# The last expert pass of a two-layer backbone step: written out, its block kept on chip and summed through fp32 weight matrices

## The reference

```python
logits = h @ router_w + router_b
top_val, top_idx = lax.top_k(logits, 2)
top_w = softmax(top_val)
for e in range(8):
    out = out + combine[..., e:e+1] * swiglu(h, w_gu[e], w_down[e])
x = layer_norm(alpha * x + gate * out, g, b)
```

## Time and profile before

| | us |
|---|---|
| median of 3 runs (1509.24 to 1511.29) | 1509.93 |
| the profiled execution | 1505.81 |
| its span, first to last instruction | 1504.2 |
| pass 7, last matmul ends | 1453.6 |
| VectorE's last instruction ends | 1497.0 |

### The profile page before, as it was taken

The page is one execution under the profiler, slowest core; times in us unless marked ns, Lnnn a source line. Parts: engine busy times, 40 slices in busy tenths (PEclk is TensorE's granted clock), DMA queues, the critical chain, the costliest instruction groups (busy, mean ns, idle before and its releaser), DMA issues.

```text
span 1504.2 us, 20810 instructions
## 1 busy us (share of the span) xinstructions
PE 1377.2 (92%) x6907; PEld 1138.0 (76%) x6907; DVE 912.4 (61%) x1197; ACT 731.1 (49%) x1125; POOL 196.9 (13%) x264
## 2 busy tenths in 40 slices
PE   6899888999999989998889999999999999999960
PEld 2766467999999879986557788888888878877850
DVE  1325557633333386225875797555557999999967
ACT  1323545233333343323444684445446888888851
POOL 1000002500000032004320725000000000000013
PEclk9899989999999999999999899999999999999985
DMA  9885553884444415446655799766667999999922
GB/s 337 264 273 199 195 185 106 298 267 125 127 126 127 131 51 143 111 165 225 240 168 169 252 387 334 244 191 228 187 190 242 374 382 379 378 381 374 378 77 90
DMA packets 255249, 342.21 MB, mean 228 GB/s; under 512 B 16927, under 2 KB 210749, under 8 KB 255053
## 3 DMA queue, kind: packets, MB, share of 16 engines
q1 hardware_dynamic: 241210, 299.55, 60.4%
q0 software_dynamic: 12688, 41.72, 7.4%
q10 hardware_dynamic: 1282, 0.04, 0.0%
HBM read 318.65 MB, written 21.55 MB: 226 GB/s over the span
## 4 chain that ended last, share of the span: by engine, by line
PE 79%; DVE 11%; ACT 4%; issue 3%; DMA 3%; SPq 1%; POOL 0%; DVEq 0%; ACTq 0%; POOLq 0%
PE PS L2061 25%; PE PS L478 15%; PE PS L2068 12%; PE PS L467 6%; PE PS L468 6%; PE PS L469 6%; DVE wlo L453 2%; PE PS L597 2%; PE PS L2036 1%; DMA raw<-in_ada_w 1%; ACT BIG L1493 1%; DVE X L772 1%; DVE BIG L767 1%; DVE stats L774 1%; PE PS L622 1%
## 5 line engine op out<-in xcount | busy, mean ns | idle before, releaser
L453 DVE TENSOR_TENSOR wlo<-raw,whi 128x1024 fp32r<-128x1024 f32 x130 | 172.2, 1351 | 230.4 <-ACT whi L450 230.0
L1926 DVE TENSOR_TENSOR wlo<-BIG,whi 128x1024 fp32r<-128x1024 f32 x192 | 239.2, 1260 | 70.7 <-ACT whi L1922 69.2
L1922 ACT ACTIVATE whi<-BIG 128x1024 fp32r<-128x1024 f32 x192 | 202.7, 1060 | 68.3 <-PE PS L2061 42.0
L2061 PE MATMUL PS<-whi,Hh 128*128 128x512 f32 x560 | 224.0, 400 | 2.3 <-DVE Hl L1983 2.2
L2061 PE MATMUL PS<-whi,Hl 128*128 128x512 f32 x560 | 219.6, 392 | 0.0
L2061 PE MATMUL PS<-wlo,Hh 128*128 128x512 f32 x560 | 219.6, 392 | 0.0
L467 PE MATMUL PS<-Hh,whi 128*128 128x384 f32 x608 | 206.8, 340 | 10.1 <-DVE Hl L757 6.5
L1926 DVE TENSOR_TENSOR wlo<-raw,whi 128x1024 fp32r<-128x1024 f32 x150 | 184.2, 1239 | 48.6 <-ACT whi L1922 47.0
L468 PE MATMUL PS<-Hl,whi 128*128 128x384 f32 x608 | 205.3, 338 | 0.0
L469 PE MATMUL PS<-Hh,wlo 128*128 128x384 f32 x608 | 205.1, 337 | 0.0
L1922 ACT ACTIVATE whi<-raw 128x1024 fp32r<-128x1024 f32 x150 | 158.5, 1059 | 58.7 <-PE PS L2068 32.3
(11 more groups left out here) (354 smaller groups left out, 1949.0 us busy)
## 6 DMA issues: line engine op xcount, KB each, us to landing
raw<-in_moe_w_gu SPq DMA_DIRECT2D x224, 256.0 KB, 5.9
BIG<-in_moe_w_gu SPq DMA_DIRECT2D x224, 256.0 KB, 6.0
raw<-in_ada_w SPq DMA_DIRECT2D x96, 512.0 KB, 4.5
BIG<-in_moe_w_down SPq DMA_DIRECT2D x80, 512.0 KB, 7.3
raw<-in_ffn_w_gu SPq DMA_DIRECT2D x44, 512.0 KB, 3.9
raw<-in_w_in_c SPq DMA_DIRECT2D x32, 512.0 KB, 3.9
raw<-in_moe_w_down SPq DMA_DIRECT2D x32, 512.0 KB, 7.2
scr_tok<-BIG POOLq DMA_DIRECT2D x29, 512.0 KB, 9.3
```

Of the source, the lines that this page charges most:

```text
L453: self.eng.tensor_tensor(wlo[:, s, :], raw[:, s, :], whi[:, s, :].bitcast(f32), ALU.subtract).then_inc(lo_made, 1)
L1922: act.activation(whi[:, slot(v), :], moe_raw(v), ACT.Copy).then_inc(hi_made, 1)
L1926: dve.tensor_tensor(wlo[:, slot(v), :], moe_raw(v), whi[:, slot(v), :].bitcast(f32), ALU.subtract).then_inc(lo_made, 1)
L2061: last = pe.matmul(PS[:, 6 * b + c % 2, :], lhs, wt[:, s, 512 * k:512 * k + 512], start=(q == 0 and k == 0 and lhs is h and wt is whi), st ...
```

## The change

The last single pass (n) leaves the loop and is written out for every engine, and its 128 results never go to DRAM. What it computes is the same.

- `pool_table` also computes for each token copy its place relative to the last block (`slf`): at least `FAR` if it lies in that block, less if not. Five more GpSimd instructions, ahead of those that make `ctl`.
- `pool_pick`, on GpSimd ahead of the loop of single passes: `e2` is the weight of each copy that lies in another block, and zero otherwise; `pick_n` is per tile a 128x128 matrix of weights from the token to its row of the last block. In the last pass TensorE transposes the three matrices (unit 20) and ScalarE copies them to `pick` (unit 22).
- In the last pass nothing is fetched, no tokens are transposed or split, and the last six splits are left out.
- Once the block of pass n-1 is stored, GpSimd gathers five of the six tiles of rows, during the last pass; the sixth when its buffer (a ring buffer) has been read. Rows that lie in the last block are multiplied by the zero in `e2`.
- ScalarE weights tile 0, 1, 2 at units 33, 36, 38 (`act_weight`). VectorE does `mix_step` (weighted add, gate, ALPHA-add into X) one or two at a time at units 36 to 41, behind the other work of the unit, and the last two steps after the pass.
- The last block's result is read from PSUM twice: by ScalarE as it is (`yb[0]`, for the context tile) and by VectorE times the latent gate (`yg`). Six fp32 matmuls of 512 columns bring it to the tokens (`pick` x `yb` or `yg`), and `last_sum` adds it to X from PSUM. The sum of the other rows is in X already.
- `last_norm`: the whole normalisation on VectorE, as two scalar-tensor-tensor instructions per tile (tile 2 in two halves, each stored by itself). GpSimd has no part in the end.

```diff
@@ buffers
-        Yg = area([128, TT, 2, D], 3072)
+        pick_n = area([128, TT, 128], 1536)
+        pick = area([128, TT, 128], 16088)
+        pick_tmp = area([128, 128])
+        Yg = [[hsn[0], hsn[1]], [yb[1], gate_bc[:, 0, 0, :]], [gate_bc[:, 0, 1, :], xraw[0]]]
+        yg = xraw[2]
@@ pool_table
+            ch.step(pool.tensor_scalar(over, cd, 256.0, -FAR, ALU.mult, ALU.add))
+            ch.step(pool.tensor_scalar(over2, cs, 128.0, None, ALU.mult))
+            ch.step(pool.tensor_tensor(over, over, over2, ALU.add))
+            for kk in range(2):
+                last = pool.tensor_tensor(slf[:, :, kk:kk + 1], wk[:, kk, :, 0:1],
+                                          over[:, 7:8].unsqueeze(1).to_broadcast([128, TT, 1]), ALU.subtract)
+            ch.step(last)
@@ new
+        def pool_pick(pool, ch):
+            ch.step(pool.tensor_scalar(e2, slf, FAR, None, ALU.is_lt))
+            ch.step(pool.tensor_tensor(e2, e2, wts[:, :, :], ALU.mult))
+            for t in range(TT):
+                for kk, dst in ((0, pick_n[:, t, :]), (1, pick_tmp)):
+                    last = pool.tensor_scalar(dst, C("iota_far"), slf[:, t, kk:kk + 1], wts[:, t, kk:kk + 1],
+                                              ALU.is_equal, ALU.mult)
+                ch.step(last)
+                ch.step(pool.tensor_tensor(pick_n[:, t, :], pick_n[:, t, :], pick_tmp, ALU.add))
+            pool.sem_inc(route_step, 1)
@@ act_pass
-                act_unit_hi(act, w + RING, p)
+                if not last or w + RING < UB:
+                    act_unit_hi(act, w + RING, p)
+                if last and w == 22:
+                    act.wait_ge(route_step, 7)
+                    act.activation(pick.rearrange("p t n -> p (t n)"), PS[:, 4, 0:TT * 128], ACT.Copy
+                                   ).then_inc(route_step, 1)
+                if last and w in (33, 36, 38):
+                    act_weight(act, (33, 36, 38).index(w))
...
+            if last:
+                act.wait_ge(yb_free[0], p + 1)
+                act.activation(yb[0][:, 0:512], PS[:, 2, :], ACT.Copy).then_inc(last_raw, 1)
+                act.wait_ge(last_gated, 1)
+                act.activation(yb[0][:, 512:D], PS[:, 3, :], ACT.Copy).then_inc(last_raw, 1)
+                return
@@ dve_pass
-                dve_unit_lo(dve, w + RING, p)
+                if not last or w + RING < UB:
+                    dve_unit_lo(dve, w + RING, p)
+                if last and w >= UB - RING:
+                    for i in LAST_MIX[w - UB + RING]:
+                        mix_step(dve, ch, i // 3, i % 3)
...
+            if last:
+                dve.wait_ge(unit_used, p * UB + (U_MOE + UB))
+                dve.tensor_tensor(yg[:, 512:D], PS[:, 3, :], gate_bc[:, 1, 0, 512:D], ALU.mult).then_inc(last_gated, 1)
+                dve.wait_ge(last_raw, 1)
+                dve.tensor_tensor(yg[:, 0:512], PS[:, 2, :], gate_bc[:, 1, 0, 0:512], ALU.mult).then_inc(last_gated, 1)
+
+        LAST_MIX = ((0,), (1,), (2, 3), (4,), (5,), (6,))
+
+        def mix_step(dve, ch, t, i):
+            y = Yg[t][0]
+            if i == 0:
+                dve.wait_ge(y_mixed, t + 1)
+                ch.step(dve.scalar_tensor_tensor(y, Yg[t][1], e2[:, t, 1:2], y, ALU.mult, ALU.add))
+            elif i == 1:
+                ch.step(dve.tensor_tensor(y, y, gate_bc[:, 1, 1 if t == 0 else 0, :], ALU.mult))
+            else:
+                dve.wait_ge(x_done, 2 * TT + t + 1)
+                ch.step(dve.scalar_tensor_tensor(X[:, t, :], X[:, t, :], ALPHA, y, ALU.mult, ALU.add))
+
+        def last_sum(dve, ch, t):
+            dve.wait_ge(y_summed, t + 1)
+            src = PS[:, (4, 6, 0)[t]:(4, 6, 0)[t] + 2, :].rearrange("p a n -> p (a n)")
+            if t == 0:
+                ch.step(dve.tensor_tensor(Yg[0][0], src, gate_bc[:, 1, 1, :], ALU.mult))
+                src = Yg[0][0]
+            ch.step(dve.tensor_tensor(X[:, t, :], X[:, t, :], src, ALU.add))
+            for half in range(2):
+                last = dve.bn_stats(stats[:, t, half, :], X[:, t, 512 * half:512 * half + 512])
+            ch.step(last)
+            dve.bn_aggr(mv[:, t, :], stats[:, t, :, :].rearrange("p a b -> p (a b)")).then_inc(var_made, 1)
+
+        def last_norm(dve, ch, t, cols):
+            dve.wait_ge(rstd_made, TT * 3 + t + 1)
+            for lo, hi in cols:
+                x = X[:, t, lo:hi]
+                ch.step(dve.scalar_tensor_tensor(x, x, mv[:, t, 0:1], lng[:, lo:hi], ALU.subtract, ALU.mult))
+                dve.scalar_tensor_tensor(x, x, rstd[:, t:t + 1], lnb[:, lo:hi], ALU.mult, ALU.add).then_inc(x_done, 1)
@@ pe_pass and pe_experts
+                if final and w == 20:
+                    pe.wait_ge(route_step, 6)
+                    for t in range(TT):
+                        last = pe.transpose(PS[:, 4, 128 * t:128 * t + 128], pick_n[:, t, :], C("ident"))
+                    last.then_inc(route_step, 1)
...
-            with pe.Fori(n2 + 1, n + 1) as p:
+            with pe.Fori(n2 + 1, n) as p:
                 pe_pass(pe, p, False, (0,), n2)
+            pe_pass(pe, n, False, (), n2, final=True)
+            pe.wait_ge(route_step, 8)
+            for t, bank, y in ((0, 4, yb[0]), (1, 6, yg), (2, 0, yg)):
+                for half in ((0, 1) if t == 0 else (1, 0)):
+                    if t == 0:
+                        pe.wait_ge(last_raw, half + 1)
+                    elif t == 1:
+                        pe.wait_ge(last_gated, 2 - half)
+                    last = pe.matmul(PS[:, bank + half, :], pick[:, t, :], y[:, 512 * half:512 * half + 512],
+                                     start=True, stop=True)
+                last.then_inc(y_summed, 1)
@@ pool_experts
+            pool_pick(pool, ch)
-            with pool.Fori(n2 + 1, n + 1) as p:
+            with pool.Fori(n2 + 1, n) as p:
...
+            for t in range(TT - 1):
+                for kk in range(2):
+                    gather(t, kk)
+            gather(TT - 1, 0)
+            pool.wait_ge(lo_made, n * UB + (S_MOE + UB - MRING + RING + 1))
+            pool.sem_inc(pool_pass, 1)
+            gather(TT - 1, 1)
@@ tail_dve
-            dve_norm_sum(dve, ch, 3, 0, mixed(dve, ch, 0))
-            dve_norm_sum(dve, ch, 3, 1, mixed(dve, ch, 1))
-            dve_norm_scale(dve, 3, 0)
-            dve_norm_sum(dve, ch, 3, 2, mixed(dve, ch, 2))
-            dve_norm_scale(dve, 3, 1)
-            dve_norm_scale(dve, 3, 2)
...
+            mix_step(dve, ch, 2, 1)
+            mix_step(dve, ch, 2, 2)
             dve.wait_ge(ln_in, 32 * 4)
+            last_sum(dve, ch, 0)
+            last_sum(dve, ch, 1)
+            last_norm(dve, ch, 0, OUT_COLS[0])
+            last_sum(dve, ch, 2)
+            last_norm(dve, ch, 1, OUT_COLS[1])
+            last_norm(dve, ch, 2, OUT_COLS[2])
@@ tail_pool
-            pool_norm(pool, ch, 3)
```

More of the change, by code:

```diff
@@ L1689, in backbone_step @@
         y_mixed = sem("y_mixed")
-        x_last = sem("x_last")
+        last_raw = sem("last_raw")
+        last_gated = sem("last_gated")
+        y_summed = sem("y_summed")
         pool_pass = sem("pool_pass")
@@ L1902, in sp_experts @@
                         sp.dma_start(dst, src).then_inc(moe_full[v % MRING], 16)
-            for v in range(RING):
-                sp.wait_ge(lo_made, n * UB + (S_MOE + UB - MRING + v + 1))
-                sp.sem_inc(moe_full[v % MRING], 32)
         def full_value(v):
@@ L1939, in gu_cols, with act_pass @@
             return xx[:, 2 * (c % 2):2 * (c % 2) + 2, 256:384]
-        def act_pass(act, p, twin, nxt):
+        def act_pass(act, p, twin, nxt, last=False):
             blocks_ = range(2 if twin else 1)
@@ L1992, in act_experts, with dve_pass @@
                 act_pass(act, p, True, (0, 1))
-            with act.Fori(n2 + 1, n + 1) as p:
+            with act.Fori(n2 + 1, n) as p:
                 act_pass(act, p, False, (0,))
-        def dve_pass(dve, p, twin, nxt):
+            act_pass(act, n, False, (), last=True)
+        def dve_pass(dve, p, twin, nxt, last=False, ch=None):
             blocks_ = range(2 if twin else 1)
@@ L2025, in dve_experts, with pe_pass @@
                 dve_pass(dve, p, True, (0, 1))
-            with dve.Fori(n2 + 1, n + 1) as p:
+            with dve.Fori(n2 + 1, n) as p:
                 dve_pass(dve, p, False, (0,))
-        def pe_pass(pe, p, twin, nxt, n2=None):
+            dve_pass(dve, n, False, (), True, ch)
+        def pe_pass(pe, p, twin, nxt, n2=None, final=False):
             blocks_ = range(2 if twin else 1)
@@ L2144, in pool_experts, with gather @@
                 stored(0, p + 1)
-            pool.wait_ge(tok_turned[0], n + 2)
+            def gather(t, kk):
+                pool.indirect_dma_start(Yg[t][kk], None, tok,
+                                        bass.IndirectOffsetOnAxis(ap=slot_u[:, t, kk:kk + 1], axis=0)
+                                        ).then_inc(y_back[t], 16)
+            pool.wait_ge(tok_turned[0], n + 1)
             pool.sem_inc(pool_pass, 1)
```

(40 more changed lines are left out.)

2 lines of the change are left out of this document (1 added, 1 removed).

## The result

The changed kernel takes 1486.8 us (median of 4 runs, 1485.27 to 1488.8) beside 1509.59 for the kernel before on the same chip: a ratio of 0.985, 95% interval 0.9832 to 0.9867, 22.8 us faster. The profiled execution took 1488.8.

The account below looks back on a forecast made before the run. The prediction took TensorE's matmuls to bound the passes and VectorE most of the tail. Span 1504.2 - 18.25 + 0.3 = 1486.2; 1.6 more gave 1487.8 profiled, 4.1 more the median 1491.9 us; range 1488 to 1497.5.

Parts of the forecast that it names:

- VectorE's queue: From the last split on, VectorE has work without a break and ends at 1478.75 instead of 1497.00.
- The 7.2 us behind VectorE's end: At the span's end: the 7.2 us stay; the last transfer of 256 KB instead of 512 gives at most 0.4.
- Sum of the end: In the tail: VectorE ends at 1478.75 instead of 1497.00, taking 18.25 us off the span.
- The early cost, 0.3: In the routing table: five GpSimd operations added ahead of the scatter cost 0 to 0.8 us, taken as 0.3.
- 5 us of slack for the token fetch: In pass 0: block 1's tokens landed at 893.3 and were wanted at 898.3, 5 us to spare.
- The pick matrices: At the start of the single passes: eleven GpSimd operations, about 6 us together, cost 0, upper end 3.
- The weight matmuls: In the tail on TensorE: one fp32 matmul at 0.86 us, the other five at 1.72 each, all hidden.
- Gathers: In the last pass: five issued about 1403, wanted at 1442, the sixth at 1449.5; cost 0, upper end 6.9 us.
- Both rivals: Gathers starve the weight stream, up to 1499, chance 0.07; the written-out pass stalls on instruction fetches, 1521, chance 0.03.
- The range: Whole kernel: 1488 to 1497.5 us; the forecast itself, 1490 to 1493.5, had a chance of 0.60.
- better: In the last pass and tail: mixes begin before the last splits delay them, shorter last transfer; 1488 to 1490, chance 0.13.

Follow-up runs that it names:

- Experiment 2: The kernel before with only the last normalisation moved to VectorE, tile 2 in two halves: 1497.45 us, ratio 0.9914.
- experiment 3: The changed kernel plus one 128x8 GpSimd memset after VectorE's last instruction: 1495.17 us, ratio 0.9897.
- experiment 4: The changed kernel plus one 128x8 GpSimd memset once the norm of tile 0 is done: 1486.18 us, ratio 0.9857.
- 9: The changed kernel with all nine mix steps on VectorE after the last pass: 1492.48 us, ratio 0.9885.
- experiment 1: The changed kernel with the five GpSimd instructions for `slf` moved behind the scatters: 1488.27 us, ratio 0.986.
- experiments 6: The kernel before with only the scatters moved ahead of the list of passes: 1505.44 us, ratio 0.9976.
- experiment 7: The changed kernel with the `slf` instructions moved behind the scatters and the scatters ahead of the list of passes: 1481.81 us, ratio 0.9823.
- Experiment 8: Experiment 7 with the nine mix steps spread over the last pass: 1481.42 us, ratio 0.9822.

## Why the prediction was right in kind and wrong in size

The profiles carry only the part of the difference that lies behind the start of the last pass; by step:

- *VectorE's queue* (I said 1478.75, which is 86.55 us behind the start of the last pass). Measured 1484.71 - 1399.47 = 85.2. The last lower split ended at 54.6 where I had 54.9; from it to the end 30.7 instead of 31.65. Each term came out within 0.2 us of its price, most a little below it; the weighting stood at 1449.12, 1452.52 and, last, 1456.56 without a wait for a gather.
- ***The 7.2 us behind VectorE's end: the failed step.*** I wrote that they "stay (the last transfer is 256 KB instead of 512, worth at most 0.4)". They did not stay: 2.5 us after. What ended the span before was not the transfer but GpSimd's drain, 8.1 us behind its last addition; it held the end up by 3.9 us, and the shorter transfer gave 0.8, twice my "at most". Experiment 2 takes both away (7.2 to 2.4), experiment 3 brings the drain back with one instruction of 0.10 us (end of the pass 8.0 longer), experiment 4 hides it. This is 4.7 of the 6.0 us by which I undersized the gain at the end. The rows of it were in the trace of before; I had followed the chain to the last instruction and did not ask who ended the span.
- *Sum of the end*: 18.25 + 4.7 + 1.3 = 24.3, as measured. Taken from the median, 1509.93 - 24.3 = 1485.6; measured 1486.8 and, in another batch, 1484.5.
- *The early cost, 0.3.* Its working was unsafe, and it is probably too low. I read 5 us of slack for the token fetch off one profile; in the second profile of the same code there is none, and TensorE waits 2.8. The three profiles with the old table (two of before, experiment 2) show waits of 0, 2.8 and 2.8 us; the changed kernel's two show 3.9 and 2.7, its variants in experiments 3, 4 and 9 drew 7.4, 0.8 and 7.1. The lengths behind the start of the last pass hardly vary, so for each batch the gain at the end, from the profiles, less the gain of the medians is what the part ahead lost: 1.6 and, in the second batch, -0.9 us for the changed kernel, and 1.5, 1.4 and 1.7 in experiments 3, 4 and 9. The middle one is 1.5 us; the intervals of the ratios leave each of them uncertain by 2 to 3.5 us. How much of it comes from the five instructions isn't settled: moving them gained nothing (2.6 us by the same sum in experiment 1), removing the whole list from ahead of the scatters did (experiments 6 and 7).
- *The pick matrices.* I took 6 us from rows and 0 on the path. After, they take GpSimd 16.4 us (1166.76 to 1183.2), and begin so:

```profile
1166.76 0.35 POOL L1875 TENSOR_SCALAR BIG<-BIG 128x6 f32<-128x6 f32 x1 [8.12 <-DMA scr_tok<-BIG]
...
1167.51 4.23 POOL L1879 TENSOR_SCALAR BIG<-cst,BIG,wts 128x128 f32<-128x128 f32 x2
1171.82 1.04 POOL L1882 TENSOR_TENSOR BIG<-BIG 128x128 f32<-128x128 f32 x1
```

  The Trainium skill, SBUF — State Buffer, "Who interferes with whom", has the two kinds of instruction exclude each other; my estimate from it was that each of the eleven could wait out a split, some 14 us more than the 6. The trace agrees in kind: about 10 more. On the path it cost nothing, as forecast: TensorE's waits for VectorE between 950 and 1380 us are the same 1.1 and 0.2 us in both kernels.
- *The weight matmuls.* The windows after, in us of the span: length, busy us of TensorE, its weight loads, VectorE, ScalarE, GpSimd (instructions), granted clock, DMA share, GB/s.

```profile
1462.00:1464.00 2.00, 0.50 (x2) 0.00 (x0) 1.84 (x3) 0.00 (x0) 0.00 (x0) 0.86 0.04 8
1464.00:1470.00 6.00, 4.86 (x6) 2.18 (x7) 5.86 (x7) 1.88 (x2) 0.00 (x0) 0.50 0.00 0
1470.00:1472.00 2.00, 2.00 (x5) 0.57 (x3) 1.97 (x4) 0.41 (x2) 0.00 (x0) 0.93 0.00 0
```

  Behind one matmul and a pause of 2.6 us the clock was at 0.50, the 1.2 GHz level, until about 1470 and rose again while they ran: 7.1 us for five, where I had 8.6. The last ended at 1472.2, and its sum was wanted at 1476.56. Hidden, as forecast.
- *Gathers and the written-out pass.* Five gathers at 1410.81 to 1418.25, the sixth at 1444.21; no split of the last pass waited for a transfer, and TensorE went from the loop into the written-out pass without a gap. Both rivals fell.
- *The range.* Its lower end, 1488.0, left 4 us for "better", and I named only earlier mixes and a shorter transfer. Experiment 8 shows that earlier mixes are worth nothing, and the shorter transfer was worth 0.8. The real surprise, a whole engine's drain, was in no rival.

Open: why experiment 2's median gains 3.4 us more than its trace; why the drain is 8.1 us in one case and 9.3 to 10.1 in others; what sets the number of slow rows in the table (15 to 25 of 55 to 59 over the profiles that have all of it ahead of the scatters). What makes a row slow, the traces do show. I take the rows of the table that are one instruction, without the memsets, in all twelve profiles, and call 0.9 us or more slow: 207 of them began while VectorE was at a split (`wlo`), and 196 of those were slow; 353 met no split at all, and the longest of those took 0.40; the other 46 began outside a split and met one before they ended, and 8 of those were slow.

The best version run is experiment 7, 1481.81 us, 0.9823 of before (experiment 8, at 1481.42, can't be told from it).

## What to carry to other kernels

Ask who ends the span before you give its last microseconds to the last transfer: look at each engine's drain, and let GpSimd issue nothing in the last 10 us or so. Issue what the next stage waits for (here the scatters) ahead of bookkeeping that nobody needs yet. One profile is one draw: the 1392 us ahead of the last pass moved by 7 us between two profiles of the same code, that pass and its tail by 0.2, so compare the lengths of stages, and read slack from more than one profile.

## What the runs showed of the hardware

GpSimd's drain at the program's end lasted 8.1 us behind a 128x1024 addition, 10.1 behind a 128x8 memset (in two runs, both records 10170 ns), and behind the issue of an indirect DMA 10.1 (1445.99 to 1456.05, after) or 9.3 (1472.08 to 1481.4, experiment 2). Small GpSimd instructions of 0.2 us took 1.0 to 1.3 when they began beside one of VectorE's splits (196 of 207), and in 353 cases away from them at most 0.40; how many are slow changes from run to run; the whole table varied from 33.0 to 45.4 us.
